# A two-block transformer kernel on one core: the layer norm of the spatial gating is taken earlier, in the loop over the heads

## The reference

```
h = rmsnorm(x); proj = h @ w_in            # ten parts of 1024 columns
q, ffwd, fbwd, i, ga, u, v, gb, ma, mb = split(proj)
y_a = hgrn2(q, ffwd, fbwd, i, ga)          # 8 heads of 128, decay products over log2 levels
# spatial gating:
v = layernorm(gelu(v), ln_w, ln_b)         # mean and variance over all 1024 channels of v
mixed = einsum('gts,bnsgc->bntgc', w_s, v per chunk of 128 positions) + b_s
y_b = gelu(u) * mixed * silu(gb)
merged = sigmoid(ma) * (y_a @ w_proj_a) + sigmoid(mb) * (y_b @ w_proj_b)
x = x + merged @ w_out                     # then a final rmsnorm, then the second block
```

## Time and profile before

| | |
|---|---|
| median of 3 runs | 1554.28 us (1553.24 to 1554.75) |
| the profiled execution | 1552.44 us, of which the span is 1550.6 us |
| PE busy | 1480.1 us (95%) |
| DVE busy | 790.0 us (51%) |
| ACT busy | 670.7 us (43%) |
| POOL busy | 556.8 us (36%) |
| granted TensorE clock, mean | 0.985 |

### The profile page before, as it was taken

The page is one execution under the profiler, slowest core; times in us unless marked ns, Lnnn a source line. Parts: engine busy times, 40 slices in busy tenths (PEclk is TensorE's granted clock), DMA queues, the critical chain, the costliest instruction groups (busy, mean ns, idle before and its releaser), DMA issues.

```text
span 1550.6 us, 22035 instructions
## 1 busy us (share of the span) xinstructions
PE 1480.1 (95%) x8808; PEld 1245.6 (80%) x8808; DVE 790.0 (51%) x1500; ACT 670.7 (43%) x1105; POOL 556.8 (36%) x488
## 2 busy tenths in 40 slices
PE   6999999999989999999999999999998997999997
PEld 5888988888867888888778988766787875888876
DVE  2868268275486324551366312777523545555533
ACT  6333344333333341223551213777723534777752
POOL 3534233323334374445424233333432241222241
PEclk9999999999999999999999999999998998999999
DMA  6533324224212135533221120200021121001011
GB/s 219 177 109 110 115 76 137 82 90 140 70 49 61 55 139 182 167 109 136 70 81 55 55 91 1 76 21 22 13 72 55 30 70 24 18 10 37 28 55 55
DMA packets 134918, 122.48 MB, mean 79 GB/s; under 512 B 17844, under 2 KB 130624, under 8 KB 134816
## 3 DMA queue, kind: packets, MB, share of 16 engines
q1 hardware_dynamic: 134702, 121.04, 24.9%
q10 hardware_dynamic: 114, 0.03, 0.0%
HBM read 116.60 MB, written 2.10 MB: 77 GB/s over the span
## 4 chain that ended last, share of the span: by engine, by line
PE 83%; DVE 12%; ACT 2%; issue 1%; POOL 0%; SPq 0%; DMA 0%; DVEq 0%; ACTq 0%
PE ps L2184 10%; PE ps L2186 10%; PE ps L2185 10%; PE ps L2507 3%; PE ps L2684 3%; PE ps L2673 3%; PE ps L2245 3%; PE ps L2498 3%; PE ps L2405 3%; PE ps L2404 3%; PE ps L2406 2%; PE ps L2273 2%; DVE q_two L1487 2%; PE ps L2176 2%; PE ps L2177 2%; PE ps L2178 2%
## 5 line engine op out<-in xcount | busy, mean ns | idle before, releaser
L1242 POOL TENSOR_TENSOR w_lo<-raw,w_hi 128x512 fp32r<-128x512 f32 x320 | 423.4, 1354 | 651.5 <-ACT w_hi L733 640.8
L2184 PE MATMUL ps<-h_hi,w_hi 128*128 128x512 f32 x632 | 253.2, 401 | 8.2 <-DVE u_g L1686 4.8
L2186 PE MATMUL ps<-h_hi,w_lo 128*128 128x512 f32 x632 | 247.2, 391 | 0.0
L2185 PE MATMUL ps<-h_lo,w_hi 128*128 128x512 f32 x632 | 247.1, 391 | 0.0
L733 ACT ACTIVATE w_hi<-raw 128x2048 fp32r<-128x2048 f32 (+1 forms) x77 | 145.5, 1890 | 126.7 <-PE ps L2186 52.0
L2184 PEld LDWEIGHTS ps<-h_hi,w_hi 128*128 128x128 f32 x632 | 119.4, 189 | 37.2 <-issue 12.4
L2186 PEld LDWEIGHTS ps<-h_hi,w_lo 128*128 128x128 f32 x632 | 119.2, 189 | 25.8
L2185 PEld LDWEIGHTS ps<-h_lo,w_hi 128*128 128x128 f32 x632 | 119.5, 189 | 23.5 <-issue 0.2
L2070 DVE CUSTOM_DVE_ANT_0 prob_b<-ps,no_mask 128x768 f32<-128x768 f32 x64 | 61.3, 958 | 37.4 <-PE ps L2663 36.3
L2176 PE MATMUL ps<-w_hi,h_hi 128*128 128x256 f32 x256 | 73.6, 287 | 0.0
L2177 PE MATMUL ps<-w_lo,h_hi 128*128 128x256 f32 x256 | 72.4, 283 | 0.0
(11 more groups left out here) (459 smaller groups left out, 3540.5 us busy)
## 6 DMA issues: line engine op xcount, KB each, us to landing
raw<-in_w_in_dram SPq DMA_DIRECT2D x32, 1024.0 KB
raw<-in_ada_w_dram SPq DMA_DIRECT2D x12, 1024.0 KB
raw<-in_a_w_in_dram SPq DMA_DIRECT2D x10, 1024.0 KB
raw<-in_w_in_dram SPq DMA_DIRECT2D x16, 512.0 KB
ada_strip<-in_ada_w_dram SPq DMA_DIRECT2D x7, 1024.0 KB, 6.5
ada_half<-in_ada_w_dram SPq DMA_DIRECT2D x10, 512.0 KB, 4.2
raw<-in_b_w_in_dram SPq DMA_DIRECT2D x5, 1024.0 KB
raw<-in_w_proj_a_dram SPq DMA_DIRECT2D x4, 1024.0 KB
```

The costliest lines, as they stand in the source:

```text
L1242: last = nc.gpsimd.tensor_tensor(w_lo[:, ph.w(s), p], raw[:, s % 2, p], w_hi[:, ph.w(s), p].bitcast(F32), ALU.subtract)
L2184: mm(ps[:, j, :], wh[:, k, c], xh[:, k, :], start=(k == 0), stop=False)
L2185: mm(ps[:, j, :], wh[:, k, c], xl[:, k, :], start=False, stop=False)
L2186: last = mm(ps[:, j, :], wl[:, k, c], xh[:, k, :], start=False, stop=(k == KT - 1))
```

## The change

`norm_v()`, `scale_v()` and `offsets()` are called in DVE's `head_tiles` at `tt` = 8, ahead of the wait for `s_gla`: the offsets in pair 1, the other two in pair 3, when all of `v` is there. ACT's Sqrt goes to `head_tiles`, pair 3, `tt` = 8, behind `gla_act(2, 8)`. The steps within `norm_v` are chained by `s_ln` in place of the helper `link`, so the counts of that semaphore are 3 (ready for the Sqrt) and 4 (Sqrt done). The first `combine` waits for a third count of `s_wsum`, which the offsets give. Nothing is computed in another way.

```diff
@@ ACT, head_tiles
                         if not first:
                             gla_act(it - 1, tt)
+                        if it == PAIRS - 1 and tt == 8:
+                            act.wait_ge(s_ln, 3)
+                            nc.scalar.activation(v_rstd[:, :], v_stat[:, :, 1], ACT.Sqrt).then_inc(s_ln, 1)
@@ ACT, gates
-                    if tt == 0:
-                        act.wait_ge(s_ln, 1)
-                        nc.scalar.activation(v_rstd[:, :], v_stat[:, :, 1], ACT.Sqrt).then_inc(s_ln, 1)
@@ DVE, now ahead of head_tiles
+            def norm_v():
+                for n in range(NT):
+                    last = v.bn_aggr(v_stat[:, n, :], v_bn[:, n, :].rearrange("p (i c) -> p i c", c=6))
+                last.then_inc(s_ln, 1)
+                dve.wait_ge(s_ln, 1)
+                v.tensor_scalar(v_rstd[:, :], v_stat[:, :, 1], LN_EPS, None, ALU.add).then_inc(s_ln, 1)
+                dve.wait_ge(s_ln, 2)
+                v.reciprocal(v_stat[:, :, 1], v_rstd[:, :]).then_inc(s_ln, 1)
+            def scale_v():
+                dve.wait_ge(s_ln, 4)
+                for n in range(NT):
+                    v.tensor_scalar(vs[:, n, :], vs[:, n, :], v_stat[:, n, 0:1], v_rstd[:, n:n + 1],
+                                    ALU.subtract, ALU.mult).then_inc(s_vs, 1)
+            def offsets():
...
+                last.then_inc(s_wsum, 1)
@@ DVE, head_tiles
                             if tt == 8:
-
+                                if it == 1:
+                                    offsets()
+                                if it == PAIRS - 1:
+                                    norm_v()
+                                    scale_v()
                                 dve.wait_ge(s_gla, 13 * g + 11)
@@ DVE, combine
                 if g:
                     dve.wait_ge(s_ybl, g)
+                else:
+                    dve.wait_ge(s_wsum, 3)
@@ DVE, gates
-                    if tt == 0:
-                        norm_v()
-                    if tt == 1:
-                        scale_v()
                     if j == 0:
-                        if g == 1:
-                            offsets()
```

More of the change, by code:

```diff
@@ L1517, in gla_out @@
                 dve.wait_ge(s_y, g + 2)
+            def norm_v():
[12 more added lines that the diff above has]
+            def offsets():
+                dve.wait_ge(s_lnp, 16)
+                dve.wait_ge(s_wsum, 2)
+                for g in range(GCH):
+                    last = v.scalar_tensor_tensor(bs_all[:, g, :], ws_sum[:, g, :], ln_cols[:, GCH + g:GCH + g + 1], bs_all[:, g, :],
+                                                  ALU.mult, ALU.add)
+                last.then_inc(s_wsum, 1)
             def ada_half(i):
@@ L1642, in combine @@
                 v.tensor_tensor(tmp[:, 3, :], tmp[:, 3, :], u_g[:, :], ALU.mult).then_inc(s_yb, 1)
[L1644 to L1663, removed]
             dve.wait_ge(s_free, gates.t0)
```

## The result

| | before | changed |
|---|---|---|
| median | 1553.76 us (4 runs, 1553.24 to 1554.75) | 1544.69 us (4 runs, 1543.47 to 1545.11) |
| profiled span | 1550.6 us | 1543.0 us |
| granted clock, mean | 0.985 | 0.984 |

The ratio is 0.9939, with a 95% interval of 0.9924 to 0.9953: faster by 9.1 us, 7 to 12 by the interval. The forecast was 9.0 us and 1545.3 us. All medians and ratios in this document leave out two executions of the kernel before, of 2116 and 2466 us, whose granted clock was 0.65 and 0.56 where it was 0.98 in the others.

What follows compares the result with a forecast made beforehand. PE, busy 95% of the span, bounds the kernel. Waits of 2.54 + 0.15 + 4.23 us, 0.3 and 0.78 of step 2 and mix(0), and 1.1 of tile 3 sum to 9.0: 1554.28 to 1545.3 us, range 1541.5 to 1549.

Steps and rivals of the forecast that it cites:

- (a): Gates, gla step 2: the keys' copies end near 424.8 us, so PE's wait of 2.54 us is gone.
- (b): Gates tile 2: u_g ends near 427.2 us and PE starts at 427.35 instead of 430.27, 2.9 us ahead.
- (c): mix(0): the 4.23 us wait for `vs` and the half clock behind it go; 7.95 us ahead.
- (d): Tile 3: tile 1's bank is free 0.7 us early; 5.46 us instead of 6.56; tile 4 starts near 441.35.
- (e): Gates: removing the 2.18 us of offsets gains nothing on PE, as the combine behind them is needed at tile 6 only.
- (f): From tile 4 on all shifts as one; the 3.83 us wait ahead of tile 6 and its half clock stay.
- The heads: Heads of pair 3: Sqrt done at 383.7 us, scaling takes 3.2, 3.6 to 7.4 us of cover; cost on PE 0.
- the ends of 2.18 and 10.7: Heads of pair 1: offsets take 2.18 us beside an idle POOL, 10.7 alternating with POOL's burst; cost 0 either way.

Runs made afterwards that it cites:

- stats_only: Against the kernel before: only statistics and Sqrt moved into the heads, scaling and offsets left in the gates; ratio 0.9974, 1548.4 us.
- offsets_only: Against the kernel before: only the offsets moved into the heads, statistics, Sqrt and scaling left in the gates; ratio 1.0006, 1553.7 us.
- no_offsets: The changed kernel with its offsets back in gates tile 2; ratio to the kernel before 0.9946, 1544.9 us.
- hi_early: The changed kernel with ACT's high half of strip 3, and so POOL's burst, taken earlier, behind the sigmoid of gates tile 3; 0.9943, 1544.4 us.
- sqrt_again: The changed kernel with a second Sqrt of the same values on ACT in gates tile 0, bringing back two table loads; one run, 1543.2 us.
- poly_first: The changed kernel with the gelu's polynomial ahead of the slot's work in all gates tiles with j = 0 but tile 14; 0.9963, 1548.3 us.
- pad12: The changed kernel with 12 more VectorE instructions between Sqrt and scaling in the heads of pair 3; ratio to the kernel before 0.9933, 1543.4 us.
- pad28: The changed kernel with 28 more VectorE instructions between Sqrt and scaling in the heads of pair 3; ratio to the kernel before 0.9999, 1553.5 us.
- poly_2468: The changed kernel with the gelu's polynomial ahead of the slot's work in gates tiles 2, 4, 6 and 8; 0.9929, 1541.7 us.
- poly_tile4: The changed kernel with the gelu's polynomial of gates tile 4 ahead of the doubling of slot 3; ratio to the kernel before 0.9936, 1543.1 us.

## Why the prediction was right, and where it was not

(a) and (b), the keys and tile 2: the keys' copies ended at 424.68 (forecast 424.8), u_g at 427.06 (427.2), tile 2 began at 427.20 (427.35). stats_only shows these steps alone.

(c) and (d), mixing product and tile 3: the product was reached at 432.9 (433.05), L1690's counterpart ended at 433.18 (433.0 to 433.4), tile 4 began at 441.01 (441.35). The lead is 9.38 us by the chain, where 9.0 was summed. The median fell by 9.1 us, and to tile 6 by the ruler it is 9.29 us.

(e) is the step that failed. It said that the offsets gain nothing because the combine behind them is needed at tile 6 only. But on DVE they also stand ahead of u_g of tile 2, which frees the bank of tile 4. In the kernel before that bank was free 2.5 us early, and offsets_only confirms a worth of zero; once PE is 9 us earlier and the burst lies over them, no_offsets puts them at 2.3 us. In the changed kernel that bank was free only 1.1 us before PE asked for it (u_g ended at 439.66, tile 4 began at 440.77 in PE's timeline). The prediction does not price it, so that it was free in time is luck. The sum came out right all the same, because it followed a chain with the offsets gone: a change that left them in the gates would have been forecast 2.3 us too high by (e), by the profile.

(f) held: the wait of 3.83 us and its collision moved with the chain, to the hundredth. The collision was a little larger: 1.8 us by subtraction in the prediction, 2.2 us by hi_early (slot 3's doubling and copy, 6.2 against 4.0 us). The half clock behind the wait was put at the length it had before; it was so in the second profile and longer in the first. That cost 1.0 of the 1.8 us by which the span of the first profile falls short of the chain's 9.4 us; the rest was lost behind the merge, at the half clock near 745 us. So one sign of being wrong that the prediction names, a gates' end that does not move by the same 9 us as tile 4, was near: it moved by 8.4 us in the first profile, and the stretch from tile 10 to the merge shrank by 9.3 us in the second.

The heads: the scaling took 2.98 us (3.2), began at 383.68 (383.7), cover 7.68 us (7.4). The statistics took 1.5 us rather than a little over 1: one tiny instruction took 0.60 us beside POOL's burst (374.77 to 380.02 us), where it took 0.17 us in the gates beside an idle POOL. The offsets took 6.27 us, between the ends of 2.18 and 10.7.

The two rules of the Trainium skill. The longest of the eight offsets took 1.38 us, just one of POOL's four (5.44 / 4 = 1.36), which is how the lock in SBUF — State Buffer, section Who interferes with whom, would show; but the median was 0.85 us, and the whole was 6.27 us, far from the bound of 10.7 us that full alternation gives. For the drain of 1.38 us behind a table load that ScalarE: Activation LUTs, section What ACT_TABLE_LOAD costs, adds, sqrt_again is a second case without it: the load ends at 426.67 and the sigmoid starts at 426.68.

## What to carry to other kernels

Work that one engine does while another waits for it can be moved into a wait as long as the wait's end is set elsewhere; the cover is the idle time that is left behind it (7.68 us here: 5.51 us more cost nothing, 12.89 us more cost 10), and it is worth measuring by padding, because a step pushed past it may also meet a burst of another engine. Parts of such a move are not additive: the last one, worth nothing alone, kept 2.3 us of what the others had won, by the profile. And before moving a step ahead of another, list everything that the other one issues, the first instruction too: `gla_init` cost 5 us in poly_first.

## What the runs showed of the chip

The same wait ahead of the same tile, of 3.83 or 3.84 us, was followed by some 3.4 us of half clock in seven profiles (the kernel before, the changed one again, offsets_only, stats_only, sqrt_again, pad12, pad28) and by 6.8 us in one, the first of the changed kernel. A wait of 2.43 us there was followed by 3.4 us of it in poly_2468, one of 2.44 us by none in poly_tile4. Other places with equal code had half clock in one profile and not in the next. Runs of the changed kernel in one group lay between 1540.29 and 1547.40 us.

VectorE's products of two SBUF tiles of 128x512 take 0.69 us alone and 1.78 us in POOL's burst. Those of 128x128 take 0.25 us alone (two in 0.49 us) and 1.32 us in the burst of hi_early (two in 2.63 us), and an offset takes 0.34 us at the least and 1.38 us at the most: a small instruction lost as much in absolute time, 1.0 to 1.1 us, as a large one.
